# Sigmoid-gate projections of a HGRN2/S5 mixer laid two beside each recurrent head

## The chip, the cores and the metric

The kernel runs on one core of a Trainium2 chip. Its time is device microseconds (us) from start to end, and the number used for it is the median of the runs. Five engines work side by side from queues of their own: TensorE (PE; its weight loads are shown as PEld), VectorE (DVE), ScalarE (ACT), GpSimd (POOL) and SyncE (SP), which issues nearly all DMAs. Queues meet only at semaphores, which are written out by hand in this kernel.

## The reference

One decoder layer on 16 meta tokens and 256 tokens (D = 2048), all in float32: a half-step SwiGLU FFN, a token mixer, another half-step FFN, a norm. The mixer is what matters here:

```
proj = u @ w_in                                # computed in blocks of 256 columns
q, f_logit, i_in, g_out, s5_u, gate_hg, gate_s5 = split(proj)
o    = hgrn2(silu(q)/sqrt(128), log f, 1 - f, i_in)       # 12 heads of 128, gated recurrence
o    = o * rsqrt(mean(o*o, per head) + eps)
o    = o * hg_norm * silu(g_out)
y_hg = o @ hg_w_proj
y_s5 = (z @ glu_a) * sigmoid(z @ glu_b)                   # z = gelu(s5(s5_u))
mix  = (sigmoid(gate_hg) * y_hg + sigmoid(gate_s5) * y_s5) @ w_out
```

The columns `g_out` (1536 of them) make 6 blocks of 256, and the two merge gates (2 x 2048) make 16: 22 blocks in all.

## The kernel before

**Weights.** Every weight matrix streams through SBUF in units of 512 rows x 256 columns (512 KB, four per column block). A unit passes three steps: SP loads it into `raw[slot]` (L259), ACT rounds it to fp32r into `w_hi` (`split`, L575), DVE takes the remainder into `w_lo` (`split`, L870). PE (`unit`, L350 to L352) then does three matmuls for each 128x128 tile: w_hi x_hi, w_hi x_lo, w_lo x_hi. A unit has 24 matmuls, a block 96. There are four slots, and `split(q, j)` prepares the unit three ahead of unit j of block q, so a unit is ready well before PE comes to it if ACT and DVE keep their place.

**A head.** `score` (L490 on) turns the values (L494, L495), and multiplies keys and queries level by level (L497 to L515) into PSUM banks 4 to 7. It waits for the semaphore `levels`, which DVE sends when it has made the scaled queries and keys of that head (`head_levels`: L1121, L1124, seven times L1112 to L1116, and L1132 at the end). DVE masks and sums the scores (`masked`, L1144 and L1147, once for each half of the tokens). `mix` (L523 to L527) makes the head's output; ACT squares it (L780), POOL makes the inverse root, ACT scales it (L786), `back` (L533) turns it on PE, and ACT takes it to `qfv` (L792), times `hg_norm`.

**The order of work around the change.** PE's loop over the twelve heads is: `score`, one column block with `mix` behind its second unit, `back`. DVE's turn for a head is: `masked` twice, all of `head_levels` of the next head, then four `split`s. So six `g_out` blocks and the first six gate blocks lie beside the twelve heads. Ten gate blocks follow in a loop of their own (L545 on), and beside the first eight of them ACT and DVE gate the head outputs, three heads at a time (L816, L1179, L1182, L819, L1188). Then come the four GLU passes, the projection, the output product and the second FFN. All engines follow the code order; no scheduler moves anything.

Of the kernel before, what the change touches and what calls it, by code (L numbers as in the profile page):

```python
# [33 lines left out]
GA = HEADS - HG_BLOCKS  # L34
GB = GATES - GA

# [6 lines left out]
Q_GATES = Q_HEADS + HEADS  # L43
Q_GLU = Q_GATES + GB
# [10 lines left out]
M_GATES = M_HEADS + HEADS  # L55
# [30 lines left out]
def program(nc, xT, metaT, gains, ffn1, w_in, hg_lb, hg_norm, w_proj, s5v, s5b, s5c, s5d, w_glu, w_out, ffn2, outT):  # L86
# [7 lines left out]
    with top:  # L94
# [72 lines left out]
        os = at(HEADS * T, "os", [P, HEADS, 2, SEQ], f32r)  # L167
        o_hi, o_lo = os[:, :, 0, :], os[:, :, 1, :]
        gates_b = at(HD, "gates_b", [P, 2 * GB, SEQ])
        sgs = at(HD + 5120, "sgs", [P, 3, SEQ])  # L170
        y_a = at(QFV + 5120, "y_a", [P, 8, SEQ])
        y_b = at(HD + 5120, "y_b", [P, 8, SEQ])
# [157 lines left out]
        def _(pe):  # L330
# [3 lines left out]
            def unit(j, u, banks, n, rhs, start, stop, need=None, wide=False):  # L334

                pe.wait_ge(lo_ready, u + RING + 1)
                by_column = [(c, k) for c in range(2) for k in range(KT)]
                by_row = [(c, k) for k in range(KT) for c in range(2)]
                for c, k in by_column if need is None else by_row:  # L340
                    if need is not None and c == 0:
                        pe.wait_ge(x_ready, need + k + 1)
                    out = ps[:, banks + c, 0:n]
                    hi, lo = w_hi[:, j, k, c * P:(c + 1) * P], w_lo[:, j, k, c * P:(c + 1) * P]
                    x = rhs(k)
                    if wide:
                        pe.matmul(ps[:, banks + c, 0:2 * n].rearrange("p (s t) -> p s t", s=2), hi, x,  # L347
                                  start=start and k == 0, stop=False)
                    else:
                        pe.matmul(out, hi, x[:, 0, :], start=start and k == 0, stop=False)  # L350
                        pe.matmul(out, hi, x[:, 1, :], start=False, stop=False)  # L351
                    last = pe.matmul(out, lo, x[:, 0, :], start=False, stop=stop and k == KT - 1)  # L352
                last.then_inc(unit_done, 1)
# [5 lines left out]

            def rows(parts, first, c0, n):  # L360
                return lambda k: parts[:, first + k, :, c0:c0 + n]
# [10 lines left out]
            def one_pass(index, q, groups, parts, c0, n, need, free=None, wide=False):  # L372

                def quad(g, start, stop):
                    need(g)
                    for j in range(4):
# [4 lines left out]
                        def rhs(k):  # L381
                            if isinstance(g, int):
                                return parts[:, 4 * g + k, :, c0:c0 + n]
                            return parts[:, ds(g * 4 + k, 1), :, c0:c0 + n].rearrange("p a s t -> p (a s) t")
# [105 lines left out]
            def score(hd):  # L490
# [9 lines left out]
                for b in range(2):  # L500
# [35 lines left out]
            def head(hd):  # L536
                score(hd)
                pe.wait_ge(block_out, hd + M_HEADS)
                column_block(hd + Q_HEADS, 0, META, DT, lambda j: mix(hd) if j == 1 else None)
                back(hd)  # L540

            with pe.Fori(0, HEADS) as hd:
                head(hd)

            with pe.Fori(0, GB // 2) as i:  # L545
                for c in range(2):
                    pe.wait_ge(block_out, i * 2 + M_GATES + c - 1)
                    column_block(i * 2 + Q_GATES + c, 2 - 2 * c, META, DT)

            pe.wait_ge(block_out, M_GATES + GB)  # L550
            for index in range(PASS_GLU, PASS_PROJ):
                one_pass(index, Q_GLU + index - PASS_GLU, 1, zs, 0, SEQ, lambda g: pe.wait_ge(z_ready, 1))
            for p in range(2):
                one_pass(PASS_PROJ + p, Q_PROJ + 3 * p, 3, os, 0, SEQ, lambda g: pe.wait_ge(o_ready, 4))
# [7 lines left out]
        def _(act):  # L562
# [204 lines left out]
            def beside_head(hd, out, func, following):  # L767
# [21 lines left out]
                split(hd + Q_HEADS, 3)  # L789
                take_block(hd + M_HEADS, out, 0, SEQ, func)  # L790
                act.wait_ge(ot_psum, hd + 1)
                act.activation(qfv[:, ds(hd, 1), META:T].rearrange("p a t -> p (a t)"), ps[:, 7, 0:SEQ], ACT.Copy,  # L792
                               scale=hgn[:, ds(hd, 1)]).then_inc(ot_done, 1)
                if following:
                    split(hd + Q_HEADS + 1, 0)

            split(Q_HEADS, 0)
            act.wait_ge(small_in[3], 16)
            with act.Fori(0, HG_BLOCKS) as hd:
                beside_head(hd, gout[:, ds(hd * 2, 2), :], ACT.Copy, True)  # L800
            with act.Fori(HG_BLOCKS, HEADS - 1) as hd:
                beside_head(hd, gates_a[:, ds(hd * 2 - HEADS, 2), :], ACT.Sigmoid, True)
            beside_head(HEADS - 1, gates_a[:, HEADS - 2:HEADS, :], ACT.Sigmoid, False)

            def gate_pair(i, c, side=None):
                for j in range(4):
                    split(i * 2 + Q_GATES + c, j)
                    if side:
                        side(j)
                take_block(i * 2 + M_GATES + c, gates_b[:, ds(i * 4 + 2 * c, 2), :], 2 - 2 * c, SEQ, ACT.Sigmoid)  # L810

            act.wait_ge(ot_done, HEADS + 1)
            with act.Fori(0, 4) as i:
                def side(j):
                    if j == 0:
                        act.activation(sgs[:, :, :], gout[:, ds(i * 3, 3), :], ACT.Sigmoid).then_inc(sgo_ready, 1)  # L816
                    if j == 3:
                        act.wait_ge(og_ready, i + 1)
                        act.activation(o_hi[:, ds(i * 3, 3), :], gout[:, ds(i * 3, 3), :], ACT.Copy).then_inc(ohi_ready, 1)  # L819
                gate_pair(i, 0, side)  # L820
                gate_pair(i, 1)
            gate_pair(4, 0)
            gate_pair(4, 1)
# [33 lines left out]
        def _(dve):  # L857
# [260 lines left out]
            def head_levels(hd, part):  # L1118
                if part == 0:
# [5 lines left out]
                    for i in range(3):  # L1125
                        level(i)
                else:
                    for i in range(3, 7):
                        level(i)
# [5 lines left out]
            head_levels(0, 0)  # L1135
            split(Q_REST + 1, 1)
            head_levels(0, 1)
# [4 lines left out]
            def head(hd, following):  # L1142
                def masked(b):
# [6 lines left out]
                    else:  # L1150
                        step(ins)
                dve.wait_ge(scored, hd + 1)
# [8 lines left out]
                split(hd + Q_HEADS, 3)  # L1161
                if following:
                    split(hd + Q_HEADS + 1, 0)

            split(Q_HEADS, 0)
            with dve.Fori(0, HEADS - 1) as hd:
                step.turn(hd, 40)
                head(hd, True)
            step.done(HEADS - 1)
            head(HEADS - 1, False)  # L1170

            dve.wait_ge(ot_done, HEADS + 1)
            with dve.Fori(0, 4) as i:
                step.turn(i, 1)
                g3 = gout[:, ds(i * 3, 3), :]
                split(i * 2 + Q_GATES, 0)
                dve.wait_ge(sgo_ready, i + 1)
                step(tt(g3, g3, sgs[:, :, :], MUL))  # L1179
                split(i * 2 + Q_GATES, 1)  # L1180
                step.join()
                tt(g3, g3, qfv[:, ds(i * 3, 3), META:T], MUL).then_inc(og_ready, 1)  # L1182
                split(i * 2 + Q_GATES, 2)
                split(i * 2 + Q_GATES, 3)
                split(i * 2 + Q_GATES + 1, 0)
                dve.wait_ge(og_ready, i + 1)
                dve.wait_ge(ohi_ready, i + 1)
                tt(o_lo[:, ds(i * 3, 3), :], g3, o_hi[:, ds(i * 3, 3), :].bitcast(f32), SUB).then_inc(o_ready, 1)  # L1188
                for j in range(1, 4):
                    split(i * 2 + Q_GATES + 1, j)  # L1190
            step.done(4)
            for c in range(2):
                for j in range(4):
                    split(Q_GATES + 8 + c, j)

            dve.wait_ge(block_out, M_GATES + GB)
            for index in range(PASS_GLU, PASS_PROJ):
# [6 lines left out]
                def take_b(j, y=y, p=p):  # L1205
# [4 lines left out]
                    t = DT + 8 * p + 2 * j - 2 * GA  # L1210
                    step(tt(yy, yy, gates_b[:, t:t + 2, :], MUL))
# [5 lines left out]
            for p in range(2):  # L1217
                def take_proj(j, p=p):
                    t = 8 * p + 2 * j
                    gate = gates_a[:, t:t + 2, :] if t < 2 * GA else gates_b[:, t - 2 * GA:t - 2 * GA + 2, :]  # L1220
# [221 lines left out]
```

## Time and profile before

| | |
|---|---|
| median of 3 runs | 2409.59 us (2409.5 to 2409.62) |
| profiled execution, first to last instruction (span) | 2408.2 us |
| PE busy | 2377.7 us, 99% of the span |
| DVE busy | 1537.1 us, 64% |
| ACT busy | 1041.5 us, 43% |
| twelve heads with a block each | about 1105 to 1328 us of the span |
| ten gate blocks | about 1328 to 1443 us |
| four GLU passes | from 1443 us |

The page gives the profiled execution as its span; the median of the runs stands 1.4 us above it, which is what lies around the first and last instruction, and the difference between executions. A PE that is busy is one with a matmul in its pipe; how closely matmuls follow each other is seen from their start times. All starts below are us from the start of the span.

### The profile page before, as it was taken

How to read it: one execution, taken by the hardware profiler on the slowest of the kernel's cores; microseconds unless marked ns; L12 is line 12 of the kernel's file. 1: busy time of each engine (PE TensorE's matmuls, PEld its weight loads, DVE VectorE, ACT ScalarE, POOL GpSimd, SP SyncE). 2: the span in 40 equal slices, each digit the busy share in tenths (PEclk: the TensorE clock that was granted, in tenths of full speed). 3: DMA queues.
4: the chain of work that ended last, by engine and by line, in shares of the span. 5: the costliest groups of instructions: out<-in, count | busy, mean ns of one | idle time of the engine just before them, and what ended most of it. 6: DMA issues, size and time to landing. Idle time of an engine off the chain costs nothing.

```text
span 2408.2 us, 45890 instructions
## 1 busy us (share of the span) xinstructions
PE 2377.7 (99%) x17248; PEld 2244.1 (93%) x17248; DVE 1537.1 (64%) x2022; ACT 1041.5 (43%) x1267; POOL 189.9 (8%) x258
## 2 busy tenths in 40 slices
PE   8999999999999899999999999999999999999997
PEld 8999999999999899899999999999888888888886
DVE  6555544567544667778898546657666654767655
ACT  5333333455543433335444544445444433444443
POOL 0000010499000200001000000000000000000000
PEclk9999999999999999999999999999999999999999
DMA  7555555555655444443333555565666566565663
GB/s 226 172 176 171 176 175 176 168 178 170 181 174 177 135 149 148 145 148 112 127 115 113 181 185 181 171 201 176 182 194 189 177 195 187 178 196 183 185 188 125
DMA packets 416915, 408.55 MB, mean 170 GB/s; under 512 B 19409, under 2 KB 416721, under 8 KB 416849
## 3 DMA queue, kind: packets, MB, share of 16 engines
q1 hardware_dynamic: 411856, 407.03, 55.2%
q10 hardware_dynamic: 4992, 0.60, 0.2%
q8 instruction: 46, 0.75, 0.1%
q14 instruction: 21, 0.16, 0.0%
HBM read 405.48 MB, written 2.10 MB: 169 GB/s over the span
## 4 chain that ended last, share of the span: by engine, by line
PE 96%; DVE 2%; ACT 1%; DMA 0%; issue 0%; ACTq 0%; DVEq 0%; SPq 0%
PE ps L352 31%; PE ps L350 21%; PE ps L351 20%; PE ps L347 20%; PE ps L510 1%; PE ps L458 1%; PE ps L478 1%; DVE xs L1026 1%; PE ps L515 0%; ACT xs L597 0%; DMA raw<-gate 0%; ACT scr L584 0%; DVE w_lo L870 0%; PE ps L525 0%; PE ps L524 0%
## 5 line engine op out<-in xcount | busy, mean ns | idle before, releaser
L870 DVE TENSOR_TENSOR w_lo<-raw,w_hi 128x1024 fp32r<-128x1024 f32 x765 | 946.7, 1246 | 681.8 <-ACT w_hi L575 674.3
L352 PE MATMUL ps<-xs,w_lo 128*128 128x256 f32 (+2 forms) x4416 | 1257.4, 285 | 0.0
L575 ACT ACTIVATE w_hi<-raw 128x1024 fp32r<-128x1024 f32 x765 | 805.1, 1058 | 946.8 <-PE ps L352 942.3
L350 PE MATMUL ps<-xs,w_hi 128*128 128x272 f32 (+2 forms) x3008 | 865.0, 288 | 11.7 <-DVE xs L1026 5.7
L351 PE MATMUL ps<-xs,w_hi 128*128 128x272 f32 (+2 forms) x3008 | 860.9, 286 | 0.0
L352 PEld LDWEIGHTS ps<-xs,w_lo 128*128 128x128 f32 x4416 | 833.2, 189 | 0.0
L350 PEld LDWEIGHTS ps<-xs,w_hi 128*128 128x128 f32 x3008 | 567.1, 189 | 28.3 <-issue 20.1
L351 PEld LDWEIGHTS ps<-xs,w_hi 128*128 128x128 f32 x3008 | 569.6, 189 | 0.0
L347 PE MATMUL ps<-xs,w_hi 128*128 128x512 f32 x1408 | 493.3, 395 | 0.3 <-DVE w_lo L870 0.3
L352 PE MATMUL ps<-hs,w_lo 128*128 (+2 forms) x1408 | 402.6, 286 | 0.0
L347 PEld LDWEIGHTS ps<-xs,w_hi 128*128 128x128 f32 x1408 | 264.5, 188 | 61.4 <-issue 0.6
L352 PEld LDWEIGHTS ps<-hs,w_lo 128*128 128x128 f32 x1408 | 265.4, 188 | 0.0
L347 PE MATMUL ps<-hs,w_hi 128*128 (+1 forms) x704 | 248.8, 395 | 0.0
L351 PE MATMUL ps<-hs,w_hi 128*128 (+1 forms) x704 | 203.5, 289 | 0.0
L350 PE MATMUL ps<-hs,w_hi 128*128 (+1 forms) x704 | 201.9, 287 | 0.0
L347 PEld LDWEIGHTS ps<-hs,w_hi 128*128 128x128 f32 x704 | 132.1, 188 | 31.4
L350 PEld LDWEIGHTS ps<-hs,w_hi 128*128 128x128 f32 x704 | 132.8, 189 | 0.0
L351 PEld LDWEIGHTS ps<-hs,w_hi 128*128 128x128 f32 x704 | 132.7, 188 | 0.0
L638 ACT ACTIVATE hs<-scr 128x544 f32 (+3 forms) x44 | 28.4, 646 | 147.1 <-DVE scr L948 85.6
L1398 POOL TENSOR_TENSOR h<-h,scr 128x512 f32<-128x512 f32 x2 | 3.4, 1734 | 1073.7 <-DVE scr L879 1073.7
L952 DVE TENSOR_TENSOR hs<-scr,hs 128x544 f32 (+3 forms) x44 | 32.7, 743 | 43.1 <-ACT hs L638 43.1
L351 PE MATMUL ps<-os,w_hi 128*128 128x256 f32 x192 | 53.9, 281 | 0.0
(245 smaller groups left out, 1714.4 us busy)
## 6 DMA issues: line engine op xcount, KB each, us to landing
raw<-gate SPq DMA_DIRECT2D x176, 512.0 KB, 4.4
raw<-up SPq DMA_DIRECT2D x176, 512.0 KB, 3.6
raw<-down SPq DMA_DIRECT2D x176, 512.0 KB, 3.6
raw<-w_in SPq DMA_DIRECT2D x168, 512.0 KB, 3.5
raw<-w_out SPq DMA_DIRECT2D x32, 512.0 KB, 3.9
raw<-w_proj SPq DMA_DIRECT2D x24, 512.0 KB, 4.2
raw<-glu_a SPq DMA_DIRECT2D x8, 512.0 KB, 3.6
raw<-glu_b SPq DMA_DIRECT2D x8, 512.0 KB, 3.6
```

The source lines that it names most:

```text
L347: pe.matmul(ps[:, banks + c, 0:2 * n].rearrange("p (s t) -> p s t", s=2), hi, x, start=start and k == 0, stop=False)
L350: pe.matmul(out, hi, x[:, 0, :], start=start and k == 0, stop=False)
L351: pe.matmul(out, hi, x[:, 1, :], start=False, stop=False)
L352: last = pe.matmul(out, lo, x[:, 0, :], start=False, stop=stop and k == KT - 1)
L458: last = pe.matmul(ps[:, 4 + r, 0:T], st_b[32 * jj:32 * jj + 32, r, :], st_u[32 * jj:32 * jj + 32, :], start=True, stop=True)
L478: last = pe.matmul(ps[32 * jj:32 * jj + 32, 6, 0:SEQ], st_c[:, jj, r, :], sx[:, r, META:T], start=r == 0, stop=r == 1)
L510: pe.matmul(out, ks[:, k, blk[b]], queries, start=True, stop=True)
L575: act.activation(w_hi[:, slot, :, :], raw[:, slot, :, :], ACT.Copy).then_inc(hi_ready, 1)
L638: act.activation(h_hi[:, ds(b * 2, 2), c0:T], scr[:, 2:4, c0:T], ACT.Copy).then_inc(hhi_ready, 1)
L870: tt(w_lo[:, slot, :, :], raw[:, slot, :, :], w_hi[:, slot, :, :].bitcast(f32), SUB).then_inc(lo_ready, 1)
L952: tt(h_lo[:, ds(b * 2, 2), c0:T], sig, h_hi[:, ds(b * 2, 2), c0:T].bitcast(f32), SUB)\
L1026: stt(x_lo[:, k, :], scr[:, k % 4, :], gain[:, 1, k:k + 1], x_hi[:, k, :].bitcast(f32), MUL, SUB)\
```

## The change

The 22 blocks now all lie beside the heads: two beside each of heads 0 to 9 (`PAIRED`), one beside head 10 and one beside head 11. The loop of ten gate blocks is gone.

- PE: a paired head is `score`, first block (banks 0, 1) with `mix` behind its third unit, second block (banks 4, 5) with `back` behind its first unit. `score` fills the second half (banks 6, 7) first, and waits for the take-out of the block before it ahead of banks 4 and 5. Heads 10 and 11 are written out behind the loop: `score`, one block, `back`.
- ACT: `silu(g_out)` is begun as soon as the block is done (sigmoid of PSUM to `sgs`, copy to `gout`); the upper part of the gated output is taken head by head (`upper_o`).
- DVE: `head_levels` is cut into four pieces with `split`s between them. DVE multiplies `gout` by the sigmoid (`silu_gate`), takes the turned head output from PSUM times `hg_norm` times the gate (`gate_o`), and the lower part (`lower_o`). `gate_o` now sends `ot_done`, which ACT sent before.
- `o_hi`, `o_lo` are two tiles; `gates_b`, `y_a`, `y_b`, `sgs` lie elsewhere.

```diff
-GA = HEADS - HG_BLOCKS
+GA = 6
+PAIRED = 10
...
+        sgs = at(HD + 5552, "sgs", [P, 2, SEQ])
+        o_hi = at(0, "o_hi", [P, HEADS, T], f32r)
+        o_lo = at(QFV + 5120, "o_lo", [P, HEADS, SEQ], f32r)
+        gates_b = qfv[:, HEADS:3 * HEADS, 0:SEQ].rearrange("p (s b) t -> p s b t", s=2)
...
@@ PE
-                for b in range(2):
+                for b in (1, 0):
+                    if b == 0:
+                        pe.wait_ge(block_out, before)
...
-            def head(hd):
-                score(hd)
-                pe.wait_ge(block_out, hd + M_HEADS)
-                column_block(hd + Q_HEADS, 0, META, DT, lambda j: mix(hd) if j == 1 else None)
-                back(hd)
-            with pe.Fori(0, HEADS) as hd:
-                head(hd)
-            with pe.Fori(0, GB // 2) as i:
-                for c in range(2):
-                    pe.wait_ge(block_out, i * 2 + M_GATES + c - 1)
-                    column_block(i * 2 + Q_GATES + c, 2 - 2 * c, META, DT)
-            pe.wait_ge(block_out, M_GATES + GB)
+            def head(hd, first, paired):
+                score(hd, first + M_HEADS)
+                pe.wait_ge(block_out, first + M_HEADS - (1 if paired else 0))
+                column_block(first + Q_HEADS, 0, META, DT, lambda j: mix(hd) if j == 2 else None)
+                if paired:
+                    column_block(first + Q_HEADS + 1, 4, META, DT, lambda j: back(hd) if j == 0 else None)
+                else:
+                    back(hd)
+            with pe.Fori(0, PAIRED) as hd:
+                head(hd, hd * 2, True)
+            for hd in range(PAIRED, HEADS):
+                head(hd, PAIRED + hd, False)
+            pe.wait_ge(block_out, M_GLU)
+            pe.wait_ge(ot_done, HEADS + 1)
...
@@ ACT, beside_head
+                split(q, 0)
                 if following:
                     act.wait_ge(levels, hd + 1)
                     head_inputs(hd + 1)
-                split(hd + Q_HEADS, 1)
+                split(q, 1)
+                split(q, 2)
                 act.wait_ge(o_done, hd + 1)
...
-                split(hd + Q_HEADS, 2)
+                split(q, 3)
                 act.wait_ge(rr_ready, hd + 1)
...
+                def take(c):
+                    if func == ACT.Copy:
+                        act.wait_ge(unit_done, (first + M_HEADS + c + Q_U) * 4 + RING + 4)
+                        act.wait_ge(og_ready, first + c + 1)
+                        act.activation(sgs[:, :, :], ps[:, 4 * c:4 * c + 2, 0:SEQ], ACT.Sigmoid).then_inc(sgo_ready, 1)
+                    take_block(first + M_HEADS + c, outs[c], 4 * c, SEQ, func)
...
+                take(0)
+                if len(outs) > 1:
+                    split(q + 1, 0)
+                    split(q + 1, 1)
+                    upper_o()
+                    split(q + 1, 2)
+                    split(q + 1, 3)
+                    take(1)
+                else:
+                    upper_o()
...
@@ DVE, head
                 masked(0)
                 step.join()
+                split(q, 0)
                 masked(1)
-                if following:
-                    head_levels(hd + 1, 0)
-                    head_levels(hd + 1, 1)
-                split(hd + Q_HEADS, 1)
-                split(hd + Q_HEADS, 2)
-                split(hd + Q_HEADS, 3)
-                if following:
-                    split(hd + Q_HEADS + 1, 0)
+                split(q, 1)
+                ahead(0, 2)
+                split(q, 2)
+                ahead(2, 4)
+                split(q, 3)
+                silu_gate(0)
+                ahead(4, 6)
+                if paired:
+                    gate_o()
+                    split(q + 1, 0)
+                    ahead(6, 7)
+                    split(q + 1, 1)
+                    lower_o()
+                    split(q + 1, 2)
+                    split(q + 1, 3)
+                    silu_gate(1)
+                else:
+                    ahead(6, 7)
+                    gate_o()
+                    lower_o()
```

`ahead(a, b)` is `head_levels(hd + 1, a, b)`: the levels a to b - 1 of the next head, with the opening two products in front of level 0 and the closing one (and the semaphore `levels`) behind level 6.

How the two queues read at the places that matter. First DVE, before, at the end of a head's turn in the loop: the last level (`ks`, `qs` and the factors `fm`), the closing product, and then the weight remainders `w_lo`.

```order
L1112 TENSOR_TENSOR ks<-ks,fm 128x2x64
L1113 TENSOR_TENSOR qs<-qs,fm 128x2x64
L1114 COPY ks<-ks 128x2x64
L1115 COPY qs<-qs 128x2x64
L1116 TENSOR_TENSOR fm<-fm 128x2
L75 REGISTER_ALU
L1132 TENSOR_SCALAR ks<-ks,fm 128x16
L869 ISA
L870 TENSOR_TENSOR w_lo<-raw,w_hi 128x1024
L869 REGISTER_ALU
L870 TENSOR_TENSOR w_lo<-raw,w_hi 128x1024
```

DVE of the changed kernel, head 10, from its start (the line numbers are those of the changed kernel; L884 is its `w_lo`):

```order
L1159 TENSOR_TENSOR prod<-ps,mask 128x768
L1162 TENSOR_REDUCE att<-prod 128x128
L884 TENSOR_TENSOR w_lo<-raw,w_hi 128x1024
L1159 TENSOR_TENSOR prod<-ps,mask 128x768
L1162 TENSOR_REDUCE att<-prod 128x128
L884 TENSOR_TENSOR w_lo<-raw,w_hi 128x1024
L1135 SCALAR_TENSOR_TENSOR qs<-qfv,scr 128x256
L1138 TENSOR_TENSOR qs<-qs,fm 128x256
```

The same head, further on, between level 3 and level 4:

```order
L1129 COPY qs<-qs 128x16x8
L1130 TENSOR_TENSOR fm<-fm 128x17
L884 TENSOR_TENSOR w_lo<-raw,w_hi 128x1024
L1126 TENSOR_TENSOR ks<-ks,fm 128x8x16
L1127 TENSOR_TENSOR qs<-qs,fm 128x8x16
```

The four `split`s of the head's block stood behind the closing product and now stand ahead of it.

PE, before, at the end of a head (`back` is L533; after the branch the loop begins again with `score`, L494):

```order
L350 MATMUL ps<-xs,w_hi 128x256
L351 MATMUL ps<-xs,w_hi 128x256
L352 MATMUL ps<-xs,w_lo 128x256
L533 MATMUL ps<-ident,scr 128x128 x2
L542 REGISTER_ALU
L542 COMPARE_AND_BRANCH
```

PE of the changed kernel, inside the second block of a paired head (`back` is L542 there):

```order
L351 MATMUL ps<-xs,w_hi 128x256
L352 MATMUL ps<-xs,w_lo 128x256
L542 MATMUL ps<-ident,scr 128x128 x2
L337 REGISTER_ALU
L350 MATMUL ps<-xs,w_hi 128x256
L351 MATMUL ps<-xs,w_hi 128x256
```

The two transposes have moved from between a block and `score` to between two units of a block.

## Rows read from the trace of the kernel before

**Rows 1.** The page: busy time and share of the span
```profile
PE 2377.7 (99%) x17248; PEld 2244.1 (93%) x17248; DVE 1537.1 (64%) x2022; ACT 1041.5 (43%) x1267; POOL 189.9 (8%) x258
```
**Rows 2.** The page: the chain that ended last, by engine
```profile
PE 96%; DVE 2%; ACT 1%; DMA 0%; issue 0%; ACTq 0%; DVEq 0%; SPq 0%
```
**Rows 3.** Windows: stretch, length, busy of PE, PEld, DVE, ACT, POOL, clock, DMA, GB/s
```profile
1105.00:1330.00 225.00, 225.00 (x1849) 210.57 (x1848) 194.42 (x515) 106.33 (x247) 14.68 (x36) 1.00 0.36 115
1330.00:1446.00 116.00, 115.31 (x970) 115.10 (x969) 60.55 (x53) 53.86 (x59) 0.00 (x0) 1.00 0.60 184
```
**Rows 4.** Timeline of DVE in one head: start, us, operation
```profile
1146.82 0.96 DVE L1144 TENSOR_TENSOR prod<-ps,mask 128x768 f32<-128x768 f32 x1 [1.52 <-PE ps L515]
...
1151.86 0.41 DVE L1121 SCALAR_TENSOR_TENSOR qs<-qfv,scr 128x256 f32<-128x256 f32 x1
...
1159.16 0.23 DVE L1132 TENSOR_SCALAR ks<-ks,fm 128x16 f32<-128x16 f32 x1
1159.31 4.62 DVE L870 TENSOR_TENSOR w_lo<-raw,w_hi 128x1024 fp32r<-128x1024 f32 x4
1165.46 0.96 DVE L1144 TENSOR_TENSOR prod<-ps,mask 128x768 f32<-128x768 f32 x1 [1.53 <-PE ps L515]
```
**Rows 5.** Timeline of PE in the same head
```profile
1146.71 0.39 PE L350 MATMUL ps<-xs,w_hi 128*128 128x256 f32 x1
...
1152.51 0.38 PE L523 MATMUL ps<-v_tok,att 128*128 128x128 f32 x2
...
1154.29 0.38 PE L350 MATMUL ps<-xs,w_hi 128*128 128x256 f32 x1
...
1160.10 0.38 PE L533 MATMUL ps<-ident,scr 128*128 128x128 f32 x2
1160.32 0.38 PE L494 MATMUL ps<-ident,scr 128*128 128x128 f32 x2
```
**Rows 6.** Timeline of ACT in the same head
```profile
1156.53 0.63 ACT L786 ACTIVATE scr<-ps,ss 128x128 f32<-128x128 f32 x2 [0.56 <-POOL ss L1391]
...
1160.40 0.60 ACT L731 ACTIVATE gout<-ps 128x512 f32 x1 [1.89 <-PE ps L352]
```
**Rows 7.** The tile gates_b: count, ns min/median/max, first and last start
```profile
L731 ACT ACTIVATE gates_b<-ps x10: 597/597/597, 1339.9 to 1442.5; 128x512 f32 x8, 128x512 f32<-128x512 f32 x2
L1211 DVE TENSOR_TENSOR y_a<-y_a,gates_b x4: 691/692/692, 1460.1 to 1468.3; 128x512 f32<-128x512 f32 x4
```
**Rows 8.** Line L1071: a three-operand product from PSUM on DVE
```profile
L1071 DVE SCALAR_TENSOR_TENSOR ys<-u,dsk,ps x4: 479/480/481, 907.3 to 1079.6; 128x256 f32 x4
```
**Rows 9.** Timeline of PE, last head into the first gate block
```profile
1327.86 0.28 PE L352 MATMUL ps<-xs,w_lo 128*128 128x256 f32 x1
...
1328.12 0.36 PE L350 MATMUL ps<-xs,w_hi 128*128 128x256 f32 x1
...
1328.32 0.28 PE L351 MATMUL ps<-xs,w_hi 128*128 128x256 f32 x1
```
**Rows 10.** Timeline of PE, last gate block into the first GLU pass
```profile
1442.21 0.28 PE L352 MATMUL ps<-xs,w_lo 128*128 128x256 f32 x1
1443.18 0.39 PE L350 MATMUL ps<-zs,w_hi 128*128 128x256 f32 x1 [0.69 <-ACT gates_b L731]
```
**Rows 11.** Windows at the opening and at the end, columns as in rows 3
```profile
7.00:8.00 1.00, 1.00 (x11) 1.00 (x10) 1.00 (x3) 0.63 (x3) 0.00 (x0) 1.00 1.08 353
...
2400.00:2402.00 2.00, 0.00 (x0) 0.00 (x0) 2.00 (x3) 0.00 (x0) 1.35 (x1) 0.50 0.49 173
```
**Rows 12.** The page: granted TensorE clock in 40 slices, 9 is full
```profile
PEclk9999999999999999999999999999999999999999
```
**Rows 13.** Timeline of PE: its start, its longest wait amid work, its last matmuls
```profile
3.65 4.99 PE L358 MATMUL ps<-ident,ones 128*128 128x128 f32 x28 [3.65 <-POOL ident L1267]
...
824.30 0.39 PE L350 MATMUL ps<-xs,w_hi 128*128 128x272 f32 x1 [2.62 <-DVE xs L1026]
...
2394.41 1.13 PE L402 MATMUL ps<-scr,ones 128*128 128x256 f32 x4 [0.92 <-ACT scr L584]
```

More of the change, by code:

```diff
@@ L487, in _, with score @@
             pe.wait_ge(ys_done, UT + 1)
-            def score(hd):
+            def score(hd, before):
                 pe.wait_ge(levels, hd + 1)
@@ L799, in _ @@
[L799 to L810, printed above, removed]
@@ new lines, in _ @@
+            with act.Fori(HG_BLOCKS // 2, (HG_BLOCKS + GA) // 2) as hd:
+                beside_head(hd, hd * 2, [gates_a[:, ds(hd * 4 + 2 * c - 2 * HG_BLOCKS, 2), :] for c in range(2)],
+                            ACT.Sigmoid, True)
+            with act.Fori((HG_BLOCKS + GA) // 2, PAIRED) as hd:
+                beside_head(hd, hd * 2, [gates_b[:, :, ds(hd * 2 + c - HG_BLOCKS - GA, 1), :].rearrange("p s b t -> p s (b t)")
+                                         for c in range(2)], ACT.Sigmoid, True)
@@ L825, in _ @@
+            for hd in range(PAIRED, HEADS):
+                beside_head(hd, PAIRED + hd, [gates_b[:, :, PAIRED + hd - HG_BLOCKS - GA, :]], ACT.Sigmoid, hd < HEADS - 1)
             for index in range(PASS_GLU, PASS_PROJ):
@@ L1124, in head_levels @@
                     step(tt(qs[:, 1, :], qs[:, 0, :], fm[:, META:T], MUL))
[L1125 to L1129, printed above, removed]
+                for i in range(first, last):
+                    level(i)
+                if last == 7:
                     step.join()
@@ L1140, in _, with head @@
             dve.wait_ge(mask_ready, 1)
-            def head(hd, following):
+            def head(hd, first, paired, silus, following):
+                q = first + Q_HEADS
                 def masked(b):
@@ L1151, in masked, with ahead, silu_gate, gate_o @@
                         step(ins)
+                def ahead(first, last):
+                    if following:
+                        head_levels(hd + 1, first, last)
+                def silu_gate(c):
+                    if silus:
+                        g = gout[:, ds(hd * 4 + 2 * c, 2), :]
+                        dve.wait_ge(sgo_ready, first + c + 1)
+                        dve.wait_ge(block_out, first + M_HEADS + c + 1)
+                        tt(g, g, sgs[:, :, :], MUL).then_inc(og_ready, 1)
+                def gate_o():
+                    dve.wait_ge(og_ready, HG_BLOCKS + 1 if not silus else first + 2)
+                    dve.wait_ge(ot_psum, hd + 1)
+                    stt(scr[:, 5, 0:SEQ], ps[:, 7, 0:SEQ], hgn[:, ds(hd, 1)],
+                        gout[:, ds(hd, 1), :].rearrange("p a t -> p (a t)"), MUL, MUL).then_inc(ot_done, 1)
+                def lower_o():
+                    dve.wait_ge(ot_done, hd + 2)
+                    dve.wait_ge(ohi_ready, hd + 1)
+                    tt(o_lo[:, ds(hd, 1), :].rearrange("p a t -> p (a t)"), scr[:, 5, 0:SEQ],
+                       o_hi[:, ds(hd, 1), 0:SEQ].rearrange("p a t -> p (a t)").bitcast(f32), SUB).then_inc(o_ready, 1)
+                dve.wait_ge(og_ready, first + 1 if silus else HG_BLOCKS + 1)
                 dve.wait_ge(scored, hd + 1)
@@ L1169, in _ @@
[L1169 to L1190, printed above, removed]
@@ new lines, in _ @@
+            dve.wait_ge(small_in[3], 16)
+            dve.sem_inc(og_ready, 1)
+            with dve.Fori(0, HG_BLOCKS // 2) as hd:
+                step.turn(hd, 40)
+                head(hd, hd * 2, True, True, True)
+            step.done(HG_BLOCKS // 2)
+            with dve.Fori(HG_BLOCKS // 2, PAIRED) as hd:
+                step.turn(hd - HG_BLOCKS // 2, 40)
+                head(hd, hd * 2, True, False, True)
+            step.done(PAIRED - HG_BLOCKS // 2)
+            for hd in range(PAIRED, HEADS):
+                head(hd, PAIRED + hd, False, False, hd < HEADS - 1)
```

86 lines of the change are left out of this document (33 added, 53 removed).

## The prediction, as put on record before the run

> **What bounds the kernel now.** I read the page first. PE is busy for 99% of the span, VectorE for 64%, ScalarE for 43% [rows 1], and the chain that ended last runs for 96% through PE [rows 2]. Only something that makes PE wait, or ends one of its waits, can move the time. So the second view is the busy time by stretch [rows 3]: from 1105 to 1330 us, the twelve heads with a block each, PE is busy for all of the 225 us; from 1330 to 1446, the ten gate blocks, for all but 0.69 us. VectorE is the fullest of the others beside the heads (194.42 of 225 us, 86%) and half idle beside the gate blocks (60.55 of 116 us). The change evens that out, but no PE time is lost to it now. The third view is the timeline of one head, engine by engine [rows 4 to 6], which gives the order and the spare time at each hand-over. The reader is to see there that VectorE closes the next head's keys and queries at 1159.16 + 0.23 = 1159.39, and PE begins that head's `score` at 1160.32: 0.93 us to spare, with the four weight remainders (4.62 us) put behind the closing product, where nobody needs them soon.
>
> **PE's own work.** The same 22 blocks, twelve `score`, `mix` and `back` are there before and after. A block alone takes 11.40 us (ten take-outs start from 1339.9 to 1442.5, nine steps) [rows 7]. In a head its two halves take 1152.51 - 1146.71 = 5.80 and 1160.10 - 1154.29 = 5.81 us, 11.61 together, 0.10 more for each return from `score` or `mix` [rows 5]; `mix` takes 1.78, `back` 0.22, and `score` about 5.0 (from 1160.32 to VectorE's next start at 1165.46, less about 0.1 for the hand-over [rows 4, 5]).
>
> What moves: in ten heads `back` goes into a block. A return to the block's matmuls is new there. Behind `back` it can be read once: from the last L352 of the last head's block to the first L351 of the gate block are 1328.32 - 1327.86 = 0.46 us [rows 9], where two steps of 0.12 and the transposes' 0.22 make 0.46, so the return costs nothing to speak of. The bounds are 0 and the 0.10 of a return from `mix`. I take 0.02 each, as the row behind `back` itself is the nearer: 10 x 0.02 = 0.2 us (0 to 1.0). `mix` one unit later, and the halves of `score` in the other order, are the same matmuls: 0.
>
> **The paired heads: does PE wait?** I lay the durations of rows 4 to 6 end to end, with t = 0 where VectorE starts on the scores. PE: block to t = 13.28 (1160.10 - 1146.82) with `mix` in it, second block with `back` to 13.28 + 11.40 + 0.22 = 24.9, then `score`. VectorE: both `masked` take 5.04 (1151.86 - 1146.82), `head_levels` 7.53 (to 1159.39), a `split` 1.155 (4.62 / 4), `silu_gate` 0.69 [rows 7], `gate_o` 0.48 (nearest row L1071, also three operands from PSUM [rows 8]). Ahead of `levels` now stand both `masked`, five `split`s, one `silu_gate`, `gate_o`: 5.04 + 7.53 + 5.78 + 0.69 + 0.48 = 19.5, and about 0.5 for `silu_gate(0)`, which waits for the first block's take-out. That is t = 20.0, against 24.9: cover 4.9 us. The whole turn of VectorE is 12.57 + 8 x 1.155 + 2 x 0.69 + 0.48 + about 0.4 for `lower_o` = 24.1 us, of a period of 18.64 + 11.40 = 30.0.
>
> Weights: unit 3 of the second block has its remainder behind `split(q + 1, 0)`, at about t = 18.9, and PE comes to it at 13.28 + 0.22 + 3 x 2.85 = 22.0: cover 3.1, the least of all units. Of DMA, a slot's next load is asked for when its remainder is made, a whole block (11 us) ahead.
>
> The new wait in `score` ahead of banks 4 and 5 is for the second block's take-out. Behind it on PE stands the rest of `score`, and then everything. ScalarE starts a take-out 0.3 us after the last matmul's start (1160.40 against 1160.10 [rows 5, 6]) and needs one pass of 0.60, or two for an output gate (sigmoid, copy): 1.5 us. PE needs for the opening of `score` and its first half about 1.2 + 1.9 = 3.1 us. Cover 1.6 us in the three heads with output gates, more in the others. The wait of `back` is covered by one more unit than it needs. So all of this costs 0.
>
> **Head 10: a stall.** Heads 10 and 11 have one block each but the new order on VectorE. PE is through its block and `back` at t = 1160.32 - 1146.82 = 13.50 and asks for `levels` of head 11. VectorE now makes all four `split`s ahead of the closing product (they stood behind it): 12.57 + 4.62 = 17.19. The ScalarE halves of these `split`s are there in time (the last, behind the squares, at about t = 12.1; VectorE asks for it at 13.2), so none of this is hidden or stretched. With 0.05 for the semaphore PE waits 17.24 - 13.50 = **3.74 us**. Bounds: 3.4, if pieces between the levels hide some of VectorE's own waits for its writes; 4.2, if each `split` alone takes its full 1.25 us. In head 9 the second block covers it; head 11 has no next head. `ot_done` of head 10 comes behind `levels`, at about 17.9, and `score` reaches its wait for it 2 us after starting: covered.
>
> In heads 10 and 11 `back` now comes one unit behind `mix`: scaled outputs are ready 1156.53 + 0.63 - 1154.29 = 2.87 us after `mix` [rows 5, 6], a unit takes 2.85 + 0.10. Cover 0.1 us; I take 0, bound 0.3 each.
>
> **Into the GLU.** Before, PE waits at the end of the gate blocks: 1443.18 - 1442.21 = 0.97 us between two starts [rows 10]. After, it waits at the same place for the last block's take-out and for `gate_o` of head 11, which comes behind the transposes: 0.12 + 0.22 + 0.2 to the end of the pipe + 0.48 = 1.0 to 1.1. I take +0.1 (0 to 0.3). Work that vanished from the gate blocks (L816, L1179, L1182, L819, L1188) was hidden under PE: 0, and so is what VectorE gains from `gates_b` and `y_a` lying elsewhere.
>
> **Sum.** 0.2 + 3.74 + 0.1 = 4.0 us on the profiled 2408.2 gives 2412.2; with the 1.4 us by which the median stands above the span, 2413.6.
>
> **Rivals.** (a) The clock falls in the stall. PE is idle in head 10 for about 3.5 us. The longest wait amid work in the trace is 2.62 us [rows 13], and the clock stays full in its slice [rows 12]; at the end, PE idles from 2395.5 and the granted clock reads 0.50 from 2400 on, 1.2 of 2.4 GHz [rows 11, 13]. The stall lies between these two, nearer the first. The opening shows what the lower level costs: 28 matmuls take 4.99 - 0.28 = 4.7 us [rows 13], and at the 11 per us that come from 7.0 on [rows 11] they would take 2.5 to 3.1, so 1.6 to 2.2 us are lost. I take 1.7, or 3.4 for twice as long. Time 2415.3 to 2417.0, slower by more than 0.2%. It decides from a fall that lasts 1.6 us. The Trainium skill (TensorE: Matmul & The Clock Gate, The HAM clock gate) says that an idle array goes to half rate and that sustained work brings it back; by that rule this case is real wherever the stall is long enough, and the trace agrees at its end.
>
> (b) A cover in the paired heads is too thin: the take-out behind the second block. It decides if ScalarE is 1.6 us later than laid out. For it: ScalarE's queue is strict, and `take(1)` stands behind `split(q + 1, 3)` and a wait. Against: ScalarE is busy 47% of the heads' time [rows 3]. A wait of 0.5 us in each of ten heads gives 2418.6.
>
> (c) The stall is not there, because VectorE runs ahead. Against: in head 10 it cannot start before the scores. Time 2409.9, no change.
>
> (d) Faster: VectorE's 86% beside the heads slows PE's matmuls by shared memory, and evening it out frees them. Against: the block's half in a head takes 5.81 us with one return in it, 5.71 without, and a half gate block, with VectorE half idle, 11.40 / 2 = 5.70. Even if 0.01 us for each of 24 half blocks were real, that is 0.2 us. If neither the stall nor the 0.97 us before the GLU were there, the sum would be 2409.6 + 0.2 - 0.97 = 2408.8, 0.03% faster and not to be told from no change. For a real gain, about 5 us, no row speaks: 2404.
>
> **How the numbers follow.** Forecast 0.62, (a) 0.12, (b) or another wait of its kind 0.13, (c) 0.09, (d) 0.04. I call 0.2%, 4.8 us, what a measurement of this kernel can tell from no change; the forecast is +0.17% and so falls within it, with the limit at 2414.4. The forecast's own bounds are 3.4 + 0 + 0 to 4.2 + 1.0 + 0.3 + 0.6, so 2413.0 to 2415.7; about a sixth of its chance lies over the limit. Slower: 0.10 + 0.12 + 0.12 = 0.34, minus little; I say 0.33. Faster 0.04. Within 0.2%: 0.63. The range takes in the bounds, most of (a) and half of (b), and leaves out half of (c) and all of a real gain: 2411.0 to 2417.5.
>
> **What would show it.** One wait of PE for VectorE (L1144 of the changed kernel, the closing product) of 3.5 to 4.2 us between the `back` of head 10 and the `score` of head 11; no other wait of PE over 0.3 us from the first head to the GLU; paired heads 30.0 us apart, and the granted clock 1.00 throughout. The first GLU matmul starts about 1.1 us after the last one of head 11's block. The forecast is wrong if PE waits in the paired heads, if the period differs from 30.0 by more than 0.1, or if matmuls at half rate follow the stall.

## The result: slower by 8.5 us

| | before | changed |
|---|---|---|
| median, us | 2409.62 (5 runs, 2409.5 to 2409.8) | 2418.16 (5 runs, 2416.86 to 2418.95) |
| profiled execution, span | 2408.2 | 2416.4 |
| mean granted TensorE clock in it | 0.998 | 0.994 |

The ratio is 1.0034, with a 95% interval of 1.0023 to 1.0045: slower by 0.34%. The forecast was 2413.6 us (2411.0 to 2417.5), no change to be told.

The page of the changed kernel, its first line, the granted clock in 40 slices, and the chain of waits by engine:

```profile
PE 2385.1 (99%) x17248; PEld 2250.7 (93%) x17248; DVE 1534.7 (64%) x2040; ACT 1037.5 (43%) x1265; POOL 191.1 (8%) x258
PEclk9999999999999999999999989999999999999999
PE 96%; DVE 2%; ACT 1%; issue 0%; DMA 0%; ACTq 0%; DVEq 0%; SPq 0%
```

These look like the lines of before [rows 1, 2, 12]: PE is even busier (2385.1 against 2377.7 us), with the same 17248 matmuls.
```profile
PE ps L501 <- DVE ks L1144: 3.2, 1, 3.2
PE ps L350 <- ACT qfv L742: 0.7, 1, 0.7
```

Two waits, the two that were forecast. The timeline of PE around the first (L542 is `back` of head 10, L501 opens `score` of head 11):

```profile
1422.66 0.28 PE L352 MATMUL ps<-xs,w_lo 128*128 128x256 f32 x1
1422.82 0.44 PE L542 MATMUL ps<-ident,scr 128*128 128x128 f32 x2
1426.50 0.69 PE L501 MATMUL ps<-ident,scr 128*128 128x128 f32 x2 [3.24 <-DVE ks L1144]
```

and of VectorE in head 10, from the scores to the closing product that PE waits for, with the four remainders (L884) between:

```profile
1409.58 0.96 DVE L1159 TENSOR_TENSOR prod<-ps,mask 128x768 f32<-128x768 f32 x1 [5.55 <-PE ps L524]
...
1412.18 1.23 DVE L884 TENSOR_TENSOR w_lo<-raw,w_hi 128x1024 fp32r<-128x1024 f32 x1
...
1415.76 1.22 DVE L884 TENSOR_TENSOR w_lo<-raw,w_hi 128x1024 fp32r<-128x1024 f32 x1
...
1419.66 1.22 DVE L884 TENSOR_TENSOR w_lo<-raw,w_hi 128x1024 fp32r<-128x1024 f32 x1
...
1422.48 1.22 DVE L884 TENSOR_TENSOR w_lo<-raw,w_hi 128x1024 fp32r<-128x1024 f32 x1
...
1426.21 0.23 DVE L1144 TENSOR_SCALAR ks<-ks,fm 128x16 f32<-128x16 f32 x1
```

From the scores to the end of the closing product are 16.86 us, where 17.19 were laid out. And the stretches around the wait, columns as in rows 3 (PE busy with its matmul count, ..., granted clock behind POOL):

```profile
1374.33:1404.37 30.04, 30.04 (x252) 28.83 (x251) 21.87 (x52) 13.71 (x26) 1.35 (x3) 1.00 0.46 141
1404.37:1423.20 18.83, 18.83 (x155) 17.35 (x153) 13.38 (x30) 8.80 (x21) 1.31 (x3) 1.00 0.39 118
1423.20:1426.50 3.30, 0.06 (x1) 0.00 (x0) 3.19 (x18) 0.37 (x1) 0.00 (x0) 0.79 0.68 210
1426.50:1432.50 6.00, 6.00 (x28) 4.87 (x29) 0.76 (x2) 0.42 (x1) 0.00 (x0) 0.50 0.04 10
1432.50:1438.50 6.00, 6.00 (x31) 5.70 (x31) 2.69 (x3) 1.90 (x5) 0.00 (x0) 0.50 0.00 0
1438.50:1444.50 6.00, 6.00 (x51) 6.00 (x51) 4.93 (x5) 2.12 (x2) 0.00 (x0) 0.98 0.33 98
```

The first row is a whole paired head with no idle PE. The third is the wait; the clock falls in it. Then PE runs at half rate for 12 us: 59 matmuls, where the 12 us from the same start in the kernel without the wait (late1, below) hold 103. `score` alone lasts to 1435.56, and the clock is back 3.2 us into the block behind it. From the wait to the GLU no other wait is longer than forecast; PE has 1.2 of its 2.4 GHz, and the experiments below show that this is all.

Where the 8.2 us of span went is read from four starts in each trace:

| start of | before | changed |
|---|---|---|
| `score` of head 0 | 1104.41 | 1104.03 |
| `score` of head 10 | 1290.89 | 1404.37 |
| `score` of head 11 | 1309.54 | 1426.50 |
| first GLU matmul | 1443.18 | 1451.47 |

The ten paired heads cost nothing (below). Head 10 is longer by 22.13 - 18.65 = 3.48 us. From `score` of head 11 to the GLU it is longer by 5.40 than with the same order and no fall (late1, below). The rest is -0.7, of it -0.38 already there before head 0. From the GLU to the last matmuls, 951 us, the two are the same to 0.03 us.

### The profile page after: what moved, and what is told of

It reads as the page before. It is cut to its first block, busy times and chain, and to the rows that moved or that the text cites. A ratio compares the mean times of both kernels' runs of the same rounds, so it can differ in the third digit from the quotient of the medians.

```text
span 2416.4 us, 45889 instructions
## 1 busy us (share of the span) xinstructions
PE 2385.1 (99%) x17248; PEld 2250.7 (93%) x17248; DVE 1534.7 (64%) x2040; ACT 1037.5 (43%) x1265; POOL 191.1 (8%) x258
## 4 chain that ended last, share of the span: by engine, by line
PE 96%; DVE 2%; ACT 1%; issue 0%; DMA 0%; ACTq 0%; DVEq 0%; SPq 0%
PE ps L352 30%; PE ps L350 20%; PE ps L351 20%; PE ps L347 20%; PE ps L519 2%; PE ps L465 1%; PE ps L485 1%; DVE xs L1040 1%; DVE w_lo L884 0%; PE ps L524 0%; DMA raw<-gate 0%; DVE scr L907 0%; ACT xs L608 0%; PE ps L534 0%; PE ps L533 0%
## 5 line engine op out<-in xcount | busy, mean ns | idle before, releaser
L884 DVE TENSOR_TENSOR w_lo<-raw,w_hi 128x1024 fp32r<-128x1024 f32 x765 | 949.2, 1246 | 640.4 <-ACT w_hi L586 631.7
L1159 DVE TENSOR_TENSOR prod<-ps,mask 128x768 f32<-128x768 f32 x24 | 22.9, 953 | 58.8 <-PE ps L524 58.8
```

The costliest lines, as they stand in the source:

```text
L884: tt(w_lo[:, slot, :, :], raw[:, slot, :, :], w_hi[:, slot, :, :].bitcast(f32), SUB).then_inc(lo_ready, 1)
```

## The experiments

Eight kernels were run, each beside the kernel before on the same chip (27 runs of that each time, medians 2409.68 and 2409.76). "Wait" is what the profile gives for PE's wait for the levels of head 11.

| kernel | wait, us | median, us | runs | lowest, highest |
|---|---|---|---|---|
| changed | 3.2 | 2418.16 | 5 | 2416.86, 2418.95 |
| late1 | 0.2 | 2409.42 | 10 | 2409.07, 2410.12 |
| late2 | 1.3 | 2410.91 | 10 | 2410.38, 2411.89 |
| late3 | 2.4 | 2414.71 | 10 | 2411.57, 2419.17 |
| warm | none | 2412.9 | 10 | 2412.18, 2414.62 |
| warm_behind | 2.5, and 0.7 ahead of `back` | 2418.92 | 4 | 2418.78, 2420.32 |
| before_pad | 3.1 | 2418.41 | 6 | 2414.61, 2419.43 |
| pause_glu | 0.2, and 4.1 ahead of the GLU | 2414.98 | 10 | 2414.18, 2415.98 |
| best | none | 2408.57 | 11 | 2408.33, 2409.14 |

**late1: the levels of head 11 behind one remainder instead of four.**

```diff
                 split(q, 0)
                 masked(1)
+                if not paired and following:
+                    ahead(0, 7)
+                    gate_o()
+                    for j in range(1, 4):
+                        split(q, j)
+                    lower_o()
+                    return
```

> The changed kernel, but in head 10 VectorE makes all of head 11's levels (and gate_o) behind one weight remainder instead of four. Theory (the whole loss of 8.5 us comes from PE's one wait for the levels of head 11: 3.4 us of waiting and about 5 us of half-rate clock behind it): the wait shrinks to about 0.3 us (12.57 + 1.16 + 0.05 - 13.5), no fall of the clock, 2409.6 + 0.3 = 2409.9 us, between 2409.4 and 2410.3. Rival (the paired layout itself costs the 5 us, by its extra returns, its new waits or its other addresses): about 2415.

Measured 2409.42 us, ratio 0.9999 (0.9989 to 1.0008). PE's wait by the view of waits:

```profile
PE ps L501 <- DVE ks L1144: 0.2, 1, 0.2
```

and in the timeline the starts of `score` of head 11 and of the GLU:

```profile
1423.75 0.44 PE L501 MATMUL ps<-ident,scr 128*128 128x128 f32 x2 [0.21 <-DVE ks L1144]
...
1443.32 0.36 PE L350 MATMUL ps<-zs,w_hi 128*128 128x256 f32 x1 [0.70 <-ACT qfv L742]
```

From `score` to the GLU: 19.57 us, where the changed kernel needs 1451.47 - 1426.50 = 24.97 for the same matmuls. The whole loss goes with the one wait. The paired layout, its moved `back`, its new waits and addresses cost nothing that the interval can tell.

**warm: the wait filled, not shortened.**

```diff
             for hd in range(PAIRED, HEADS):
                 head(hd, PAIRED + hd, False)
+                if hd == PAIRED:
+                    keep_warm(15, 3)
```

> The changed kernel with 15 matmuls of ones by the identity (0.216 us each, 3.2 us) on PE between back of head 10 and score of head 11; VectorE's order and so the arrival of the levels are unchanged. Theory (idle PE lets the clock fall, and the fall costs 5 us): the wait is filled, not shortened, the clock stays full, 2409.6 + 3.4 to 3.6 = 2413.1 us. Rival (the 5 us behind the wait come from something else than the clock, for instance VectorE or ScalarE being behind with the weights): 2418, as the changed kernel.

Measured 2412.9 us. PE between `back` of head 10 and `score` of head 11:

```profile
1424.02 0.44 PE L542 MATMUL ps<-ident,scr 128*128 128x128 f32 x2
1424.29 3.51 PE L358 MATMUL ps<-ident,ones 128*128 128x128 f32 x30
1427.71 0.44 PE L501 MATMUL ps<-ident,scr 128*128 128x128 f32 x2
...
1447.29 0.36 PE L350 MATMUL ps<-zs,w_hi 128*128 128x256 f32 x1 [0.70 <-ACT qfv L744]
```

and three of the windows over it and behind it:

```profile
1424.00:1427.00 3.00, 3.00 (x29) 2.98 (x28) 2.93 (x14) 0.60 (x1) 0.00 (x0) 1.00 0.62 189
1427.00:1430.00 3.00, 3.00 (x26) 2.53 (x25) 1.43 (x7) 0.42 (x1) 0.00 (x0) 1.00 0.31 104
1430.00:1433.00 3.00, 3.00 (x30) 2.65 (x30) 0.02 (x1) 0.09 (x1) 0.00 (x0) 1.00 0.00 0
```

From `back` to `score` of head 11 PE takes 3.69 us here and 3.68 in the changed kernel (0.62 in late1), so it comes as late. But the clock stays at 1.00, and from `score` to the GLU it needs 1447.29 - 1427.71 = 19.58 us, as in late1. So in the traces the wait is worth 3.1 us, and the other 5.4 come only where PE is idle in it. The medians say much the same: 2412.9 - 2409.42 = 3.5 for the wait, 2418.16 - 2412.9 = 5.3 for the rest. The rival, that VectorE or ScalarE are late behind the wait, falls.

**before_pad: the wait in the old layout.** Four idle products on VectorE ahead of the levels of head 11, in the kernel before:

```diff
                 masked(1)
+                if padded:                       # head 10 alone
+                    dve.wait_ge(att_ready, hd + 1)
+                    for _ in range(4):
+                        step(tt(prod[:, :, :], prod[:, :, :], prod[:, :, :], SUB))
+                        step.join()
                 if following:
                     head_levels(hd + 1, 0)
...
+            head(HEADS - 2, True, True)
             head(HEADS - 1, False)
```

> The kernel before, with four idle products on VectorE (128x768 each, about 1.0 us) ahead of the levels of head 11 alone, so that PE waits for them about 3.1 us in the old layout (12.57 + 4.0 + 0.05 - 13.5). Their result is used by nothing. Theory (wait plus clock, layout has no part in it): 2409.6 + 3.1 = 2412.7 with the clock full, and 2417 to 2418 if it falls; since the wait is a little shorter than in the changed kernel, the fall may come in some executions and not in others. Rival (the loss behind the wait belongs to the paired layout): 2412.7 in every run.

Measured 2418.41 us, five of six runs between 2417.69 and 2419.43, one 2414.61. The wait in its profile:

```profile
PE ps L494 <- DVE ks L1132: 3.1, 1, 3.1
```

and two stretches behind it, by windows:

```profile
1312.60:1318.60 6.00, 6.00 (x29) 4.86 (x30) 4.45 (x4) 0.00 (x0) 0.00 (x0) 0.50 0.58 167
1318.60:1324.60 6.00, 6.00 (x32) 5.70 (x32) 2.79 (x3) 0.95 (x4) 0.00 (x0) 0.50 0.54 182
```

The same wait puts the same loss on the kernel before. It belongs to the wait, not to the layout. The one run of 2414.61 shows that its size is not fixed here either.

**late2 and late3: a shorter wait.** As late1, with two and three remainders ahead of `ahead(0, 7)`.

> As late1, but with two weight remainders ahead of the levels of head 11 instead of one. PE's wait: that of late1 (0.38 us in its trace) plus one remainder of 1.16, so 1.5 us. Theory (a short wait costs its own length, and no clock): 2409.4 + 1.2 = 2410.6, clock full. Rival (the loss is proportional to the wait, 8.5 us for 3.4 of waiting): 2409.7 + 2.5 x 1.5 = 2413.4.

> As late1, with three weight remainders ahead of the levels: the wait is 0.38 + 2.32 = 2.7 us. Theory (the clock falls or not, nothing between): either 2409.4 + 2.3 = 2411.7 with the clock full, or about 2416.7 with a fall of 13.7 us; a wait of 2.9 us amid work elsewhere in this program is followed by a fall in some traces and not in others, so the runs of this kernel may spread between the two. Rival (loss proportional to the wait): 2416.3 in every run.

late2 measured 2410.91 us, 1.5 over late1 for a wait longer by 1.1, all runs within 1.5 us. In the two traces its GLU starts 1.12 us later, the length of the wait alone, with the clock at 1.00 throughout; the other 0.4 of the medians has no cause that a trace shows. late3 spread: five runs from 2411.57 to 2413.27 us, three from 2416.14 to 2416.28, two at 2418.14 and 2419.17. With 2.4 us of waiting the clock falls in some executions and not in others, and the height of the loss differs too. Only one of them has a trace, but the mean clock of each run goes with its time: 0.997 in the five short ones, 0.996 in the three middle ones, 0.994 and 0.995 in the two longest. The profiled one is a long one (2418.14):

```profile
1426.00:1429.00 3.00, 3.00 (x15) 2.22 (x16) 1.69 (x3) 0.42 (x1) 0.00 (x0) 0.56 0.17 34
1429.00:1435.00 6.00, 6.00 (x34) 5.40 (x34) 0.27 (x1) 0.34 (x2) 0.00 (x0) 0.50 0.22 73
1435.00:1441.00 6.00, 6.00 (x34) 6.00 (x34) 5.84 (x5) 2.42 (x6) 0.00 (x0) 0.58 0.23 67
```

The clock was still 1.00 through the wait and fell at about 1426.4, behind the start of `score` at 1425.89. It stayed down for 13.7 us, as long as in the changed kernel and in before_pad counted from the fall. The part of the fall that lies in the wait is free (1.4 us in the changed kernel, by the 0.79 over its 3.30 us; none here), and so `score` and its block lose 6.0 us here and 5.4 there. The loss is not proportional to the wait: that rival allowed 2416.3 in every run.

**pause_glu: the idle time ahead of dense work.** late1, with the four idle products ahead of `gate_o` of head 11, so that PE waits ahead of the GLU passes (the edit of late1 in head 10 is left out below):

```diff
                 else:
-                    ahead(6, 7)
+                    dve.wait_ge(att_ready, hd + 1)
+                    for _ in range(4):
+                        step(tt(prod[:, :, :], prod[:, :, :], prod[:, :, :], SUB))
+                        step.join()
                     gate_o()
```

> late1 with four idle products on VectorE (128x768) ahead of gate_o of head 11, so that PE is idle for about 4 us not ahead of score but ahead of the GLU passes, where dense blocks of matmuls follow. Theory (after a fall the clock comes back only when PE is filled again; score's small matmuls fill it badly, so the half-rate stretch was long, 13.7 us): behind dense work the stretch is shorter, the loss 1.7 to 3.5 us, time 2409.9 + 3.1 of waiting + loss = 2414.7 to 2416.5. Rival (a fall has one price, about 5 us, whatever follows): 2418.

Measured 2414.98 us: 5.6 over late1. Of that the start of the GLU is 3.4 late (1446.76 against 1443.32), and about 2.1 are lost behind it. The timeline at the GLU's first matmul:

```profile
1446.76 0.55 PE L350 MATMUL ps<-zs,w_hi 128*128 128x256 f32 x1 [4.07 <-issue]
```

and the windows around it:

```profile
1442.70:1446.70 4.00, 0.00 (x0) 0.00 (x0) 3.82 (x5) 0.42 (x2) 0.00 (x0) 0.74 0.42 131
1446.70:1449.70 3.00, 2.94 (x14) 2.97 (x15) 1.65 (x2) 1.36 (x2) 0.00 (x0) 0.50 0.02 5
1449.70:1452.70 3.00, 3.00 (x20) 3.00 (x20) 0.69 (x1) 0.65 (x1) 0.00 (x0) 0.70 0.55 175
1452.70:1455.70 3.00, 3.00 (x28) 3.00 (x27) 1.92 (x2) 1.22 (x2) 0.00 (x0) 1.00 0.04 10
```

The profile names no releaser for this wait (`issue`). It is longer (4.1 against 3.2 us), and yet less than half as much is lost behind it (2.1 against 5.4 us): dense blocks follow, and the clock is back within 6 us.

**warm_behind: dense work between the wait and `score`.**

```diff
             for hd in range(PAIRED, HEADS):
+                if hd == HEADS - 1:
+                    pe.wait_ge(levels, hd + 1)
+                    keep_warm(20, 3)
                 head(hd, PAIRED + hd, False)
```

> The changed kernel with 20 matmuls of ones by the identity on PE behind the wait for the levels of head 11 and ahead of its score (warm had them ahead of the wait). Theory (the clock returns when PE is filled; score's small matmuls do not fill it): the half-rate stretch shrinks from 13.7 us to about 3.4 to 6.8, PE spends 2 x 0.216 us on each matmul in it and 0.216 behind it, so 20 x 0.216 + 1.7 to 3.4 = 6.0 to 7.7 us more than no clock fall: 2409.7 + 3.4 + 6.0 to 7.7 = 2419.1 to 2420.8. Rival (a fall ahead of score lasts 13.7 us whatever PE does): 2409.7 + 3.4 + 4.3 + about 6 = 2423.4.

Measured 2418.92 us, in four runs; the expectation was 2419.1 to 2420.8, just above it, and its rival 2423.4. PE's wait and its forty matmuls in the timeline (each of the twenty is two):

```profile
1426.91 6.16 PE L358 MATMUL ps<-ident,ones 128*128 128x128 f32 x40 [2.48 <-DVE ks L1147]
```

and the windows over them:

```profile
1427.00:1430.00 3.00, 3.00 (x14) 3.00 (x15) 0.67 (x2) 0.42 (x1) 0.00 (x0) 0.51 0.03 9
1430.00:1433.00 3.00, 3.00 (x29) 3.00 (x28) 0.00 (x0) 0.00 (x0) 0.00 (x0) 1.00 0.02 5
```

The clock falls again and is back after 3 us instead of 12; `score` of head 11 and its block then take 19.50 us, as in late1. So it is what PE runs behind the fall that keeps the clock down or lifts it. It does not pay here, since the filling itself takes 1432.90 - 1426.91 = 5.99 us. The idle time is much the same as in the changed kernel: in this trace PE also waited 0.67 us ahead of `back` of head 10, as GpSimd's part of the inverse root was late (L1424 took 1.09 us, where it took 0.29 in the changed kernel).

**best: late1, and the last wait covered.** In head 11 `mix` stands behind the fourth unit, `back` behind the first unit of the GLU, and ScalarE takes the block out ahead of the squares:

```diff
-                column_block(first + Q_HEADS, 0, META, DT, lambda j: mix(hd) if j == 2 else None)
+                last = isinstance(hd, int) and hd == HEADS - 1
+                column_block(first + Q_HEADS, 0, META, DT, lambda j: mix(hd) if j == (3 if last else 2) else None)
...
-            pe.wait_ge(ot_done, HEADS + 1)
+                def free(j):                     # ahead of unit j of the first GLU pass
+                    if j == 1:
+                        back(HEADS - 1)
+                    if j == 3:
+                        pe.wait_ge(ot_done, HEADS + 1)
...
+                if last:                         # ACT
+                    split(q, 3)
+                    take_block(first + M_HEADS, outs[0], 0, SEQ, func)
                 act.wait_ge(o_done, hd + 1)
```

> late1, and in head 11 mix stands behind the fourth unit and back behind the first unit of the GLU passes, so that mix covers the take-out of the last block; ScalarE takes the block out ahead of the squares. Theory (the 0.97 us between head 11 and the GLU, which both kernels have, is a wait for the take-out and for gate_o alone): it goes, and the time is late1's 2409.4 less 0.9 to 1.0 = 2408.5 us, below both kernels. Rival (something else is then late, the weights of the first GLU pass or gate_o): 2409.4 or more.

Measured 2408.57 us. PE goes from `mix` into the GLU without a wait:

```profile
1441.30 0.48 PE L536 MATMUL ps<-v_meta,att_m 16*128 16x128 f32 x2
1441.71 0.39 PE L350 MATMUL ps<-zs,w_hi 128*128 128x256 f32 x1
```

It lies 0.85 us below late1 and 1.2 below the kernel before. Its slowest of 11 runs (2409.14) is under the fastest of the 27 beside it (2409.24), but the interval of the ratio, 0.9986 to 1.0004, takes in 1. The trace shows the wait gone; a gain of the whole is not shown.

## Why the prediction was wrong, step by step

- **What bounds the kernel, and PE's own work: right.** Paired heads were put at 30.0 us; the first row of the windows above has 30.04, and `score` starts at 1134.07 and 1164.10 in the trace. The moved `back` cost 0: 30.03 against 18.64 + 11.40 = 30.04 [rows 4, 7]. No wait in any paired head.
- **Head 10: right in place and cause, 0.3 too long.** `score` came 1426.50 - 1423.04 = 3.46 us behind `back`'s two transposes (1422.82 + 0.22; 3.24 in the row, which counts from the modelled end of the matmuls) for the 3.74 of the sum. The closing product ended at 16.86 rather than 17.19. Four remainders took 4.54 for 4.62, and the levels 7.28 for 7.53: behind `fm` a remainder starts after 0.14 us (1419.52 to 1419.66), the next level's `ks` after 0.33 (1418.50 to 1418.83). That was the case of the lower bound, 3.4. The upper bound took 1.25 us for a remainder alone; the rows have 1.22 and 1.23.
- **Into the GLU: right**, 1451.47 - 1450.26 = 1.2 us from the block's last matmul, with `back` in it (1.1 forecast, 0.97 before [rows 10]).
- **The clock behind the stall, the failed step.** The sum stopped at the wait and put nothing for a slower clock behind it; the fall was only rival (a), with a chance of 0.12 and a price of 1.7 to 3.4 us. All five runs lie at 2416.86 to 2418.95, none near 2413, and the trace has the fall: matmuls at half rate behind the stall, one of the forecast's own signs of being wrong. It costs 5.3 us (changed kernel less warm; 5.4 between traces). Two readings went wrong, the chance and the price.
- **The chance.** One wait of 2.62 us whose slice shows a full clock [rows 12, 13] was taken to speak against a fall at 3.2. A slice of 60 us could not have shown a short fall: the page of late1 has nothing but nines as well, though by windows its clock falls behind this very wait (0.82 from 822 to 826 us, 0.67 from 826 to 829). In the trace of before the clock was in fact full there, but that was the luck of one execution. The same wait of 2.62 us, at about 824 us, has a fall behind it in eight of the ten traces, that of before_pad among them, whose code up to there is the kernel before; only before and pause_glu have none. late3, at 2.4 us, falls in some runs and not in others.
- **The price.** It was read from the program's opening, from the spacing of the ones-by-identity matmuls, which quickens after 3.4 us to the 11 per us of rows 11:

```profile
3.65:7.00 3.35, 3.35 (x15) 3.35 (x16) 0.50 (x2) 1.33 (x4) 0.00 (x0) 1.00 1.09 223
```

  The clock column reads 1.00 over those 15 matmuls, so that they ran at half rate is inferred; the same matmuls in warm_behind bear it out, with 14 in 3 us at a clock of 0.51 and 29 at 1.00. In head 11 `score`'s small products follow, and the clock stays down for 12 us. warm_behind and pause_glu show that this is the difference: 3 us down behind the same dense matmuls as in the opening, about 5 behind dense blocks.
- **The rule of the Trainium skill** (TensorE: Matmul & The Clock Gate, The HAM clock gate), that idle time halves the rate and sustained work restores it, was cited and given too small a weight. This trace agrees with it: the clock is at 0.50 behind a PE that stood idle for 3.2 us, and at 0.98 once the block has run for 3 us. Case (a) with the measured 5.3 instead of 1.7 to 3.4, on the forecast less its 0.3 for the wait, would have given 2413.3 + 5.3 = 2418.6, against 2418.16 measured.
- **Rivals (b), (c), (d)**: no run bears them out. (b) needed a late take-out; there is none. (c) needed no stall; there is one. As for (d), a paired head, with VectorE at 73% (21.87 of 30.04 us), takes as long as a head and a gate block took apart, 30.04, with VectorE at 86 and 52% [rows 3].

What stays open: why late3 has two heights of loss (4.6, and 6.6 to 7.6 us over its lowest run), of which only one has a trace, and what decides whether a wait brings a fall. At 1.3 us (late2) none of ten runs shows one; at 2.4 (late3) five of ten do; at 2.62, at about 824 us, eight of ten traces do.

## What to carry to other kernels

Where PE is busy throughout, look for the hand-over that loses its cover at the end of a pattern: a new order that is right for ten paired turns was late in the one unpaired turn with a successor. In this kernel an idle PE of 2.4 us or more ahead of work that PE bounds cost its own length and, in half or all of the runs, the half-rate work behind it as well: price both, and look at what work that is. Moving three of the four remainders behind the product that PE waits for gives the whole loss back; filling the wait with matmuls gives back the 5.3 us of it that are the clock's.

## What the runs showed of the hardware

- The stretch at half rate depends on what follows the idle time: 12 us from the start of `score` (many products of 128x128 and smaller; 12 in before_pad too; 13.7 in late3, where the clock fell only behind its start), about 5 from the start of dense 128x256 blocks, 3 from that of dense 128x128 products of ones. The last two are one trace each.
- A fall need not cost anything. In the changed kernel the clock also falls at about 824 us, where the trace of before has it full. This is not the change's doing (eight of the ten traces have it, see above). PE waits there for inputs in both. The two stretches, before and then changed:

```profile
822.00:826.00 4.00, 1.70 (x13) 1.70 (x14) 4.00 (x5) 2.88 (x5) 4.00 (x5) 1.00 0.00 0
826.00:829.00 3.00, 1.58 (x13) 1.36 (x11) 3.00 (x4) 2.01 (x4) 2.62 (x4) 1.00 0.55 170
...
822.00:826.00 4.00, 2.08 (x10) 2.08 (x11) 4.00 (x5) 2.64 (x5) 4.00 (x4) 0.80 0.00 0
826.00:829.00 3.00, 2.89 (x16) 2.68 (x16) 3.00 (x5) 2.37 (x4) 2.62 (x4) 0.70 0.53 175
```

Both reach the first head at the same distance from there (within 0.01 us), the one with the clock at half for 3.4 us and the other without: PE's waits there end with VectorE's `xs` (5.7 us of them in before, 4.1 in the changed kernel), so what half rate takes comes out of the waiting.
- Two transposes between units of fp32r matmuls cost their own 0.22 us and no more; a paired head with them inside a block takes 30.03 us.
